# A routing chain that turns the unnormed tokens, and forty turns of the identity in front of the first ranks

## The reference, cut to what matters

```python
h = rms_norm_2(x, norm_moe_w_2)                # x * rsqrt(mean(x*x) + 1e-6) * w
group = h @ moe_w_group_2 + moe_b_group_2      # 8 columns
expert = h @ moe_w_expert_2 + moe_b_expert_2   # 64 columns
# per token: the best group, its two best experts, a gate for each;
# y = sum of gate * (silu(h @ w1[e]) * (h @ w3[e])) @ w2[e];  x = x + y
```

## Time and profile before

| | us |
|---|---|
| median of 3 runs | 3284.68 |
| lowest and highest | 3284.26, 3285.56 |
| profiled execution | 3284.82 |
| its span, first to last instruction | 3283.0 |
| TensorE busy in it | 3094.9 (94%) |
| VectorE, ScalarE, GpSimd busy | 1389.0, 887.1, 134.4 |

### The profile page before, as it was taken

One profiled execution on the slowest core, in us unless ns is written; L12 is line 12 of the kernel. 1 busy time (PEld: TensorE's weight loads), 2 busy tenths in 40 slices (PEclk: granted clock), 3 DMA queues, 4 the chain that ended last, 5 costly groups with the idle time before them and its releaser, 6 DMA issues.

```text
span 3283.0 us, 34804 instructions
## 1 busy us (share of the span) xinstructions
PE 3094.9 (94%) x14748; PEld 2159.3 (66%) x14748; DVE 1389.0 (42%) x2291; ACT 887.1 (27%) x1408; POOL 134.4 (4%) x118
## 2 busy tenths in 40 slices
PE   9999999999999999999999899998999889999995
PEld 7678688887677778888888787886434334434332
DVE  5675543335586553334777576434211111111112
ACT  3452322222343322222344432332111111111111
POOL 0000000001000000000211010000000000000001
PEclk9999999999999999999999999999999999999998
DMA  5122122333222222322322430235999999999997
GB/s 178 52 77 97 57 93 97 100 108 118 65 64 86 69 80 87 109 97 96 110 68 68 119 102 33 81 112 229 401 429 429 430 429 429 428 426 429 428 429 304
DMA packets 197794, 627.49 MB, mean 191 GB/s; under 512 B 11712, under 2 KB 129216, under 8 KB 172672
## 3 DMA queue, kind: packets, MB, share of 16 engines
q1 hardware_dynamic: 176288, 581.46, 45.5%
q10 hardware_dynamic: 19152, 35.61, 3.0%
q0 software_dynamic: 2192, 8.13, 0.9%
HBM read 600.26 MB, written 22.81 MB: 190 GB/s over the span
## 4 chain that ended last, share of the span: by engine, by line
PE 75%; DVE 10%; DMA 8%; ACT 3%; issue 2%; POOL 2%; ACTq 0%; SPq 0%; DVEq 0%
PE bank L121 72%; PE bank L124 3%; DMA pieces<-in_moe_w 3%; DVE gate_acc L139 2%; DMA highs<-in_moe_w 2%; DMA piece_high<-in_moe_w 2%; DVE x_tok L139 1%; POOL root L136 1%; DVE piece_rounded L136 1%; DVE stat L154 1%; ACT piece_high_rounded L127 1%; DVE probs L142 1%; DVE aprobs L142 1%; ACT probs L127 1%; DVE qs L136 1%
## 5 line engine op out<-in xcount | busy, mean ns | idle before, releaser
L136 DVE TENSOR_TENSOR piece_rounded<-piece,piece_high_rounded 128x2048 fp32r<-128x2048 f32 (+2 forms) x160 | 346.7, 2171 | 527.6 <-ACT piece_high_rounded L127 527.5
L121 PE MATMUL bank<-xT_rounded,piece_high_rounded 128*128 128x512 f32 (+1 forms) x1424 | 541.4, 380 | 12.1 <-DVE xT_low_rounded L136 7.2
L121 PE MATMUL bank<-xT_low_rounded,piece_high_rounded 128*128 128x512 f32 (+1 forms) x1424 | 538.7, 378 | 0.0
L121 PE MATMUL bank<-xT_rounded,piece_rounded 128*128 128x512 f32 (+1 forms) x1424 | 538.4, 378 | 0.0
L136 DVE TENSOR_TENSOR gate_and_hidden<-gate_and_hidden,bank 64x512 f32<-64x512 f32 x64 | 69.3, 1082 | 801.8 <-ACT gate_and_hidden L127 801.8
L127 ACT ACTIVATE piece_high_rounded<-piece 128x2048 fp32r<-128x2048 f32 (+2 forms) x160 | 288.1, 1804 | 254.6 <-DMA piece<-in_ffn_w_down 91.5
L121 PEld LDWEIGHTS bank<-xT_rounded,piece_high_rounded 128*128 128x128 f32 x1424 | 269.1, 189 | 64.2 <-DVE xT_low_rounded L136 8.2
L121 PEld LDWEIGHTS bank<-xT_rounded,piece_rounded 128*128 128x128 f32 x1424 | 269.1, 189 | 49.4
L121 PEld LDWEIGHTS bank<-xT_low_rounded,piece_high_rounded 128*128 128x128 f32 x1424 | 269.1, 189 | 48.1
L121 PE MATMUL bank<-mT_pair,xeT 128*64 128x512 f32 x352 | 178.8, 667 | 22.8 <-issue 22.8
L121 PE MATMUL bank<-xT,xeT 128*64 128x512 f32 x336 | 172.4, 673 | 23.0 <-issue 22.6
(11 more groups left out here) (344 smaller groups left out, 4903.1 us busy)
## 6 DMA issues: line engine op xcount, KB each, us to landing
mT_pair<-in_moe_w SPq DMA_DIRECT2D x32, 2048.0 KB, 16.5
pieces<-in_moe_w SPq DMA_DIRECT2D x32, 2048.0 KB, 16.5
piece_high<-in_moe_w SPq DMA_DIRECT2D x32, 2048.0 KB, 16.4
highs<-in_moe_w SPq DMA_DIRECT2D x32, 2048.0 KB, 16.7
xT<-in_moe_w SPq DMA_DIRECT2D x32, 2048.0 KB, 16.7
memory_norms<-in_moe_w SPq DMA_DIRECT2D x31, 2048.0 KB, 16.7
piece<-in_ffn_w_in SPq DMA_DIRECT2D x40, 1024.0 KB, 5.0
piece<-in_w_in SPq DMA_DIRECT2D x20, 1024.0 KB, 4.8
```

Source lines behind the costliest of these rows:

```text
L121: return self.engine.matmul(*a, **k) if self.engine is not None else Nothing()
L136: return self.engine.tensor_tensor(*a, **k) if self.engine is not None else Nothing()
```

## The change

The router's products no longer wait for the norm. `rows_to_T_pe_f32` turns `x_tok` itself, as soon as the add is done. The norm's weight is multiplied into `router_w` once (VectorE, before tile 0's norm; the weight comes in as eight more columns of `cols`), and each token's root comes in with the bias: `logits = bank * root + router_b`, one step for each tile. Tiles 0 and 1 are turned in `turned(0)`; in `turned(1)`, between the two halves of tile 3's products, TensorE makes the router products of tiles 0 and 1 and turns tile 2. Tile 3's product goes to a bank of its own. The square of tile 3 moves behind the copies of its turned rows on ScalarE, its norm row behind `both` on VectorE.

Behind the last router product TensorE turns the identity forty times into a bank that nobody reads. Then it ranks two experts alone (`first_rank`), from which VectorE makes `local` and `chosen` of the first pair; the ranks of all 64 follow, and the count stands behind the turns of the first gathered rows. The gather waits for the low part of each tile by itself. The load into `xT` comes before the one into `norms`.

```diff
         def turned(i):
-            if i:
+            if i == 0:
+                for j in (0, 1):
+                    self.rows_to_T_pe_f32(e, j)
                 return
+            self.banks.take(e, "router", 0)
             for j in (0, 1):
-                self.rows_to_T_pe_f32(e, j)
+                self.logits_pe(e, j)
+            self.rows_to_T_pe_f32(e, 2)
...
         def normed(i):
-            self.rms_dve(e, i, self.hn_low[:, i, :], self.gain[:, :], "moe_norm", ("moe_norm", "gain"), KD)
+            if i == 0:
+                e.wait_ge(*at("router_tables", "iota"))
+                e.tensor_tensor(self.router_w, self.router_w,
+                                self.cols[:, PC_NORM:PC_NORM + KD].unsqueeze(2).broadcast_to([P, KD, GROUPS + EXPERTS]),
+                                ALU.mult).then_inc(*e.tick("router_w"))
+            if i < NT - 1:
+                self.rms_dve(e, i, self.hn_low[:, i, :], self.gain[:, :], "moe_norm", ("moe_norm", "gain"), KD)
...
+        self.rows_to_T_pe_f32(e, NT - 1)
+        self.logits_pe(e, 2)
+        banks.give(("router", 0), "logits", 2)
+        banks.take(e, "router", 1)
+        self.logits_pe(e, NT - 1)
+        banks.give(("router", 1), "logits", NT - 1)
+        bank = banks.take(e, "warm")
+        for j in range(40):
+            ins = e.transpose(bank[:, j % 4 * P:(j % 4 + 1) * P], self.ident[:, :], self.ident[:, :])
+        ins.then_inc(*e.tick("pe", "warm"))
+        banks.give(("warm",), "pe", "warm")
+        bank = banks.take(e, "first_rank")
         e.wait_ge(*at("both"))
         e.wait_ge(*at("ones"))
+        e.matmul(bank[:, 0:2 * NT], self.tri, self.both[:, :, 0:2], start=True, stop=False).then_inc(*e.tick())
+        for n in range(1, NT):
+            ins = e.matmul(bank[:, 2 * n:2 * NT], self.ones, self.both[:, 0:NT - n, 0:2], start=False, stop=(n == NT - 1))
+        ins.then_inc(*e.tick("pe", "first_rank"))
...
+    def logits_pe(self, e, i):
+        W = GROUPS + EXPERTS
+        bank = self.bank("router", i // 3)
+        e.wait_ge(*self.at("router_w"))
+        for b in (0, 4):
+            e.wait_ge(*self.at("hnT", i, b))
+        for k in range(KD):
+            ins = e.matmul(bank[:, i * W:(i + 1) * W], self.xT[:, k, i * P:(i + 1) * P], self.router_w[:, k, :],
+                           start=(k == 0), stop=(k == KD - 1))
+        ins.then_inc(*e.tick("pe", "router", i))
...
-            e.wait_ge(*self.at("moe_norm", "rms", i))
-            self.transposes(e, bank, [self.hn_low[:, i, (b + j) * P:(b + j + 1) * P] for j in range(4)]).then_inc(
+            e.wait_ge(*self.at("merge_out", "added", 1, i))
+            self.transposes(e, bank, [self.x_tok[:, i, (b + j) * P:(b + j + 1) * P] for j in range(4)]).then_inc(
...
+        square(0)
+        square(1)
+        self.hn_high_act(e, 0)
+        square(2)
+        self.hn_turned_act(e, 0)
+        self.hn_turned_act(e, 1)
+        self.hn_high_act(e, 1)
+        self.hn_turned_act(e, 2)
+        self.hn_high_act(e, 2)
         self.hn_turned_act(e, NT - 1)
+        square(NT - 1)
         self.hn_high_act(e, NT - 1)
...
-        for i in range(1, NT):
+        for i in range(1, NT - 1):
             self.hn_split_dve(e, i)
-        e.wait_ge(*at("pe", "router"))
-        e.tensor_tensor(logits, self.bank("router")[:, 0:NT * W].rearrange("p (i w) -> p i w", i=NT),
-                        self.row(self.router_b, W), ALU.add).then_inc(*e.tick("logits"))
+        for i in range(NT):
+            if i == NT - 1:
+                self.rms_arg_dve(e, i, "moe_norm")
+            e.wait_ge(*at("pe", "router", max(i, 2)))
+            e.wait_ge(*at("root", "moe_norm", i))
+            e.scalar_tensor_tensor(out=logits[:, i, :], in0=self.bank("router", i // 3)[:, i * W:(i + 1) * W],
+                                   scalar=self.root[:, i, 0:1], in1=self.router_b, op0=ALU.mult,
+                                   op1=ALU.add).then_inc(*e.tick("logits", i))
...
+        self.rms_row_dve(e, NT - 1, self.hn_low[:, NT - 1, :], self.gain[:, :], "moe_norm", ("moe_norm", "gain"), KD)
+        first = self.local[:, :, 0:2]
+        e.wait_ge(*at("pe", "first_rank"))
+        e.scalar_tensor_tensor(out=first, in0=self.both[:, :, 0:2], scalar=FAR,
+                               in1=self.bank("first_rank")[:, 0:2 * NT].rearrange("p (i e) -> p i e", i=NT),
+                               op0=ALU.mult, op1=ALU.subtract).then_inc(*e.tick("first_local"))
+        e.wait_ge(*e.own())
+        self.chosen_dve(e, 0)
+        self.hn_split_dve(e, NT - 1)
...
+        self.add_slot("xT", self.xT[:, :, :].rearrange("p k s -> p (k s)"), ("pe", "router", NT - 1))
         self.add_slot("norms", memory, ("moe_norm", "rms", NT - 1), ("pe", "m_branch", "retention", KD - 1))
-        self.add_slot("xT", self.xT[:, :, :].rearrange("p k s -> p (k s)"), ("pe", "router"))
...
         self.rows_T_pe(e, 0)
+        self.count_pe(e)
         self.upper_pe(e, 0)
```

More of the change, by code:

```diff
@@ L64 @@
 PC_GATE = DEPTH * PC_LAYER
-PC_ALL = PC_GATE + 2 * KD
+PC_NORM = PC_GATE + 2 * KD
+PC_ALL = PC_NORM + KD
 SLOT = KD * BANK // 2
@@ L2461, in router_pe @@
         banks, at = self.banks, self.at
-        W = GROUPS + EXPERTS
-        bank = banks.take(e, "router")
-        e.wait_ge(*at("router_tables", "iota"))
-        for i in range(NT):
-            if i % 2 == 0:
-                self.rows_to_T_pe_f32(e, 2 + i // 2)
-            for b in (0, 4):
-                e.wait_ge(*at("hnT", i, b))
-            for k in range(KD):
-                ins = e.matmul(bank[:, i * W:(i + 1) * W], self.xT[:, k, i * P:(i + 1) * P], self.router_w[:, k, :],
-                               start=(k == 0), stop=(k == KD - 1))
-            ins.then_inc(*(e.tick("pe", "router") if i == NT - 1 else e.tick()))
-        banks.give(("router",), "logits")
-        bank = banks.take(e, "rank")
+        self.rows_to_T_pe_f32(e, NT - 1)
[10 more added lines that the diff above has]
+        bank = banks.take(e, "first_rank")
         e.wait_ge(*at("both"))
         e.wait_ge(*at("ones"))
+        e.matmul(bank[:, 0:2 * NT], self.tri, self.both[:, :, 0:2], start=True, stop=False).then_inc(*e.tick())
+        for n in range(1, NT):
+            ins = e.matmul(bank[:, 2 * n:2 * NT], self.ones, self.both[:, 0:NT - n, 0:2], start=False, stop=(n == NT - 1))
+        ins.then_inc(*e.tick("pe", "first_rank"))
+        banks.give(("first_rank",), "first_local")
+        bank = banks.take(e, "rank")
         both = self.both.rearrange("p i e -> p (i e)")
@@ L2484, in router_pe, with count_pe @@
         banks.give(("rank",), "rank_copied")
-        bank = banks.take(e, "count")
+    def count_pe(self, e):
+        bank = self.banks.take(e, "count")
         for j in range(NT):
@@ L2489, in router_pe @@
         ins.then_inc(*e.tick("pe", "count"))
-        banks.give(("count",), "counted")
+        self.banks.give(("count",), "counted")
+    def logits_pe(self, e, i):
[8 more added lines that the diff above has]
+        ins.then_inc(*e.tick("pe", "router", i))
     def rows_to_T_pe_f32(self, e, i):
@@ L2598, in router_dve, with chosen_dve @@
                                op1=ALU.subtract).then_inc(*e.tick("local"))
+    def chosen_dve(self, e, n):
+        for i in range(NT):
+            e.tensor_tensor(self.rounded(self.chosen[n // 2 % 2][:, i, :, :]),
+                            self.from_far.unsqueeze(1).broadcast_to([P, 2, CAP]),
+                            self.local[:, i, n:n + 2].unsqueeze(2).broadcast_to([P, 2, CAP]),
+                            ALU.is_equal).then_inc(*(e.tick("chosen", n // 2) if i == NT - 1 else e.tick()))
     def counts_dve(self, e):
@@ L2865, in experts_dve @@
         for n in range(EXPERTS + 1):
-            if n < EXPERTS and n % 2 == 0:
+            if 0 < n < EXPERTS and n % 2 == 0:
                 e.wait_ge(*self.at("local"))
@@ L2869, in experts_dve @@
                     e.wait_ge(*self.at("pe", "rows", n // 2 - 2, 1))
-                for i in range(NT):
-                    e.tensor_tensor(self.rounded(self.chosen[n // 2 % 2][:, i, :, :]),
-                                    self.from_far.unsqueeze(1).broadcast_to([P, 2, CAP]),
-                                    self.local[:, i, n:n + 2].unsqueeze(2).broadcast_to([P, 2, CAP]),
-                                    ALU.is_equal).then_inc(*(e.tick("chosen", n // 2) if i == NT - 1 else e.tick()))
+                self.chosen_dve(e, n)
             if n >= 1:
@@ L3186, in columns @@
     out[:, PC_GATE:PC_GATE + 2 * KD] = tile(np.asarray(inputs["b_branch_gate_2"])[0])
+    out[:, PC_NORM:PC_NORM + KD] = tile(np.asarray(inputs["norm_moe_w_2"])[0])
     return out
```

11 lines of the change are left out of this document (4 added, 7 removed).

## The result

The changed kernel takes 3291.41 us (median of 17 runs, 3287.12 to 3295.01) against 3285.56 us (17 runs) of the kernel before, measured beside it: ratio 1.0015, 95% interval 1.0008 to 1.0022. It is slower by 4.9 us by the ratio, where the prediction had it faster by 3.5. The profiled execution took 3288.2 us, its span 3286.4.

The account below looks back on a forecast made before the run. The prediction took TensorE's slot releases near 2331, set by the routing chain before them, to bound the end. Gather 1.5 us earlier plus 2.0 us from its clock made 3.5 us: 3281.2 us, 8-in-10 range 3279.6 to 3284.2.

Parts of the forecast that it names:

- Up to the gather: Routing chain from tile 3's sum to the first gather: gather starts at 2272.0 instead of 2273.51, 1.5 us earlier.
- tile 3's sum: Last token tile's sum on TensorE: ready at 2257.6 instead of 2254.0, net 3.6 us later.
- the end of the last router product: TensorE, behind tile 3's turns: ends at 2263.05 instead of 2263.55, since the norm leaves the chain.
- the end of the norm row: VectorE, tile 3, after `both`: takes 2.10 us, until 2270.8, the last thing to end before `local`.
- The small `local`: VectorE, before the first pair's `chosen`: 0.2 us, with bounds 0.15 and 0.42.
- The count: Behind the gathered rows' turns, 0.9 us beside VectorE's copies: costs nothing, or 0.2 us if not covered.
- The gather's clock: First gather: forty turns keep TensorE's clock at 1.00, fifteen steps take 3.5 us instead of 5.48, gaining 2.0 us.
- rival A: First gather: the clock falls all the same; gain only 0.7 us, time 3284.0; chance 0.12.
- Rival B: Clock falls elsewhere, before the second pair's gather, after a 3.2 us wait; 1.7 to 2.8 us lost; chance 0.18.
- Rival C: Weight stream starts 3.6 us later and DMA engines, not TensorE's releases, set the end: slower, 3288.3 us; chance 0.05.
- one for one: First expert's start to the end: any shift moves the 2331.43 release and the end equally, if loads between are in time.
- unbroken from 2328 at 428 GB/s: Weight stream of the last third: runs without a hole from 2328, back 3.5 us earlier for good.

Follow-up runs that it names:

- e14: The changed kernel, word for word, a second sample; ratio 1.0015 to the kernel before.
- e15: Changed kernel with `mean_var` behind `xT` (weight slots at old addresses), plus 24 identity turns in TensorE's pause before the third gather; 0.9994 to the kernel before.
- e3: The changed kernel without the forty turns of the identity; ratio 1.0011 to the kernel before.
- e12: The changed kernel with the weight slots at their old addresses, without the forty turns; ratio 0.9992 to the kernel before.
- e1: The kernel before with `cols` eight columns wider, in SBUF and input array; 1.0013, 3290.87 us.
- e5: The kernel before with `cols` eight columns wider in SBUF alone; ratio 1.0009.
- e13: The kernel before with `cols` 32 columns (128 bytes) wider in SBUF alone; ratio 1.0006.
- e17: The kernel before with `cols` 64 columns (256 bytes) wider in SBUF alone; ratio 0.9998.
- e6: The kernel before with the input array `cols` alone eight columns wider, nothing moved in SBUF; ratio 1.0004.
- e8: The kernel before, unchanged, a second sample; ratio 1.0004.
- e4: The changed kernel with tile 3's merge product made whole before the router products of tiles 0 and 1 and tile 2's turns; 1.0014 to the kernel before.
- e10: Changed kernel, weight slots at old addresses, tile 3's merge product made whole before the router products of tiles 0 and 1; 0.9994 to the kernel before.
- e11: Changed kernel, weight slots at old addresses, tile 3's product made whole first, VectorE's slot arithmetic after the third pair's `chosen`; 0.9983 to the kernel before, 3281.04 us.
- e9: Changed kernel, weight slots at old addresses, VectorE's slot arithmetic put after the third pair's `chosen`; 0.9990 to the kernel before.
- e7: The changed kernel with `mean_var` moved behind `xT`, so the weight slots lie at their old addresses; ratio 1.0000 to the kernel before.
- e16: The kernel before with only VectorE's slot arithmetic put after the third pair's `chosen`; ratio 0.9992.
- e18: Changed kernel, weight slots at old addresses, slot arithmetic late, tile 3's product whole first, without the forty turns; 0.9988 to the kernel before.

## Why the prediction was wrong, step by step

**Up to the gather it was right.** Foretold and measured, the latter less 0.53: tile 3's sum 2257.6 and 2257.75, its turns 2258.4 and 2258.49, the end of the last router product 2263.05 and 2263.15, the end of the norm row 2270.8 and 2270.81, the gather 2272.0 and 2271.87. The small `local` took 0.09, not 0.2. The count cost nothing: from the last gather step to the first expert it is 2.61 us in both.

**The gather's clock was mis-sized**, the term of 2.0 us. In the profiled execution it gave 1.0, in e14 it took 0.8 more than before. I had read from one stretch of the first mixer that a clock of 1.00 goes through 1.5 us of nothing, and priced rival A at 0.12. Here the wait ahead of the first ranks was 1.4 us, and the clock fell 1.5 us behind its end. That these waits bring the fall is argued from where it lies; no run closed them alone. The turns themselves did hold the clock, from 2263.5 to 2270.9 here, where it had fallen at 2267.5 before, and in the whole of e15's pause. By the Trainium skill (TensorE: Matmul & The Clock Gate, Part 4: PE-mode transpose) a transpose does not count as busy in the way a matmul does; the traces disagree, as the prediction had it. Even so the turns were not worth their 2.0 us, since without them (e3, e12) the clock fell earlier and was back earlier.

**Rival B was the likelier case**, not 0.18. The changed kernel had the fall at the third gather in every profile in which the pause was left, and it costs 1.5 us (5.13 against 3.60 us), once 2.7. I had seen the pause of 3.2 us and its clock of 1.00, from a single execution, and took this for a property of the kernel. Six more profiles of its instructions (e1, e5, e13 and e17 with the fall, e6 and e8 without) show that the instructions alone do not decide it. A and B together leave 1.1 of 3.5 us.

**Rival C had the right sign and the wrong mechanism.** Making the product whole first (e4, e10) puts the stream's start back and moves the releases by only 0.3 to 0.4 us, and e11 releases 2.0 us earlier than e9. In all three pairs the first gather ends earlier by the same 0.3 to 0.4 and 2.1 us: it starts 0.9 earlier, since the add of tile 3 hides behind the router products, and its clock makes the rest. Nothing is left for the early stream; the holes behind it only take up what was loaded before. e11 is faster than e9 by 0.0007, which is within the scatter.

**What made it slower was in no case.** The part of the change that I gave a subclause, eight more columns in `cols`, moved every buffer behind it by 32 bytes. The stretch of 907 us in which only the DMA engines count lost 0.41% of its rate, 3.7 us. The three pairs with and without the move differ by 0.0015, 0.0019 and 0.0020 (the changed kernel and e7, e3 and e12, e4 and e10), 5 to 6.6 us, each good to about 4. The profiles say it with less scatter: from the issue of `highs` near 2331 to that of the last weights it is 899.0 to 901.2 us in the eight profiles with the pause and no loss of rate, and 903.6 to 905.5 in the eight shifted by 32, 64 or 128 bytes, 4.1 us more on the mean. With the chain's -1.1 the 3.7 to 6.6 make 2.6 to 5.5, and 4.9 was measured. The step that failed is the one from the releases to the end, "one for one", with the stream "unbroken from 2328 at 428 GB/s": it puts the 907 us behind at the same length before and after, without a reason, and they became some 4 us longer. Nor does an earlier release arrive one for one where nothing is shifted: e9 and e16 give the slots back 2 to 4 us before the kernels with the pause do and issue their last load no earlier.

## What to carry to other kernels

Where a long stretch is bound by DMA, look at where the buffers stand before and after any edit that changes a size: a rate that is off by 0.4% outweighs a chain that is shorter by 3.5 us, and moving one small buffer behind the big ones gives it back. What the clock does around a pause can differ between executions of the same instructions, so price it by several profiles. Taking such a pause away by the order of VectorE's work moved the releases by more than shortening the chain in front of it; in the time the two together are clear of the scatter (e11, e18), the pause alone in the kernel before (e16) is not.

## What was not expected of the hardware

Shifting SBUF buffers by 32, 64 or 128 bytes takes the 16 KB weight packets from a mean of 612.7 ns to 615.3 to 615.6, 615.0 and 614.4, those into a slot that did not move among them, and a shift of 256 bytes leaves it at 612.7. The input array's place in device memory, moved by 4 KB, shows nothing (612.9). And the same instructions ahead of the first gather gave 4.5 us in three profiles and 6.3 to 6.4 in three others: the granted clock stood at 0.50 for 3.4 us in the changed kernel's first profile and for 6.8 in e14.
